# Macaron conv/attention layer step on one core: the first two weight tiles of the opening taken together, step by step

## The reference

```python
def rmsnorm(x, g):
    xf = x.astype(jnp.float32)
    y = xf * lax.rsqrt(jnp.mean(xf * xf, axis=-1, keepdims=True) + EPS)
    return (y * g.astype(jnp.float32)).astype(x.dtype)

def swiglu_ffn(x, norm_g, w_gu, w_down):
    h = rmsnorm(x, norm_g)
    g, u = jnp.split(h @ w_gu, 2, axis=-1)
    return (jax.nn.silu(g) * u) @ w_down

...
    x = x + 0.5 * swiglu_ffn(x, lw['norm_ffn1'], lw['ffn1_w_gu'], lw['ffn1_w_down'])
```

## Time and profile before

| | |
|---|---|
| median of 3 runs | 1531.73 us (1531.05 to 1533.61) |
| the profiled execution's own time | 1531.8 us |
| its span | 1530.0 us |
| PE busy | 1515.0 us, 99% of the span |
| DVE busy | 1031.8 us, 67% |
| ACT busy | 657.2 us, 43% |
| POOL busy | 663.8 us, 43% |
| mean granted PE clock | 0.997 |
| read from HBM | 118.31 MB |

### The profile page before, as it was taken

The page is one execution under the profiler, slowest core; times in us unless marked ns, Lnnn a source line. Parts: engine busy times, 40 slices in busy tenths (PEclk is TensorE's granted clock), DMA queues, the critical chain, the costliest instruction groups (busy, mean ns, idle before and its releaser), DMA issues.

```text
span 1530.0 us, 31753 instructions
## 1 busy us (share of the span) xinstructions
PE 1515.0 (99%) x11075; PEld 1465.3 (96%) x11075; DVE 1031.8 (67%) x1644; ACT 657.2 (43%) x1247; POOL 663.8 (43%) x679
## 2 busy tenths in 40 slices
PE   8999999999999999999999999999999999999999
PEld 8999999999999999588999999988999999999999
DVE  6998888422269975865877777864759988885000
ACT  6444345322221241364666666652434434445111
POOL 4165546445445644320233333223552654555432
PEclk9999999999999999999999999999999999999999
DMA  6233334232223341002322222312222333332322
GB/s 176 70 96 96 96 89 124 66 92 78 81 71 100 98 111 51 1 0 59 80 62 63 66 63 63 89 56 70 83 83 64 103 96 87 104 94 80 91 76 81
DMA packets 230911, 122.80 MB, mean 80 GB/s; under 512 B 28295, under 2 KB 227400, under 8 KB 230806
## 3 DMA queue, kind: packets, MB, share of 16 engines
q1 hardware_dynamic: 229950, 121.09, 28.2%
q10 hardware_dynamic: 864, 0.48, 0.1%
HBM read 118.31 MB, written 3.58 MB: 80 GB/s over the span
## 4 chain that ended last, share of the span: by engine, by line
PE 89%; DVE 5%; ACT 2%; issue 2%; POOL 1%; DMA 1%; SPq 0%; ACTq 0%; DVEq 0%; POOLq 0%
PE ps L498 39%; PE ps L1527 27%; PE ps L1907 10%; PE ps L1799 1%; PE ps L1670 1%; PE ps L1724 1%; PE ps L1699 1%; PE ps L1838 1%; PE ps L1817 1%; PE ps L1867 1%; PE ps L1818 1%; POOL w_lobuf L473 1%; PE ps L484 1%; PE ps L1714 1%; PE ps L1676 1%
## 5 line engine op out<-in xcount | busy, mean ns | idle before, releaser
L473 POOL TENSOR_TENSOR w_lobuf<-w_rawbuf,w_hibuf 128x256 fp32r<-128x256 f32 (+1 forms) x332 | 315.5, 981 | 360.3 <-ACT w_hibuf L466 360.2
L1527 PE MATMUL ps<-xs,w 128*128 128x288 f32 x3192 | 427.5, 296 | 1.9 <-DVE w L2033 1.9
L1527 PEld LDWEIGHTS ps<-xs,w 128*128 128x128 f32 x3192 | 426.8, 188 | 2.4 <-issue 2.4
L820 POOL TENSOR_TENSOR w<-w_raw,w 128x256 fp32r<-128x256 f32 x216 | 219.5, 1048 | 228.9 <-DVE w_raw L2021 149.8
L466 ACT ACTIVATE w_hibuf<-w_rawbuf 128x1024 fp32r<-128x1024 f32 (+1 forms) x89 | 104.4, 1173 | 345.9 <-PE ps L498 341.3
L2235 DVE SCALAR_TENSOR_TENSOR xT<-ps,xT 128x576 f32<-128x576 f32 x23 | 17.4, 757 | 202.4 <-PE ps L498 202.4
L498 PE MATMUL ps<-a_hi,w_lobuf 128*128 128x288 f32 x682 | 147.5, 298 | 0.0
L498 PE MATMUL ps<-a_hi,w_hibuf 128*128 128x288 f32 x682 | 147.1, 296 | 0.0
L498 PE MATMUL ps<-x_hi,w_hibuf 128*128 128x288 f32 x656 | 142.5, 299 | 4.3 <-POOL w_lobuf L473 2.5
L498 PE MATMUL ps<-a_lo,w_hibuf 128*128 128x288 f32 x682 | 145.4, 294 | 0.0
L498 PE MATMUL ps<-x_hi,w_lobuf 128*128 128x288 f32 x656 | 141.2, 297 | 0.0
(11 more groups left out here) (353 smaller groups left out, 2851.4 us busy)
## 6 DMA issues: line engine op xcount, KB each, us to landing
w_raw<-in_ffn_w_gu SPq DMA_DIRECT2D x76, 256.0 KB, 2.9
up_rows<-in_ffn_w_gu SPq DMA_DIRECT2D x72, 256.0 KB, 3.2
c_nat<-in_cache_ckv SPq DMA_DIRECT2D x128, 128.0 KB, 2.0
w_rawbuf<-in_w_in SPq DMA_DIRECT2D x58, 256.0 KB, 3.2
w_rawbuf<-in_ffn_w_down SPq DMA_DIRECT2D x32, 384.0 KB, 4.1
w_rawbuf<-in_ffn_w_down SPq DMA_DIRECT2D x32, 320.0 KB, 3.4
w_rawbuf<-in_ffn_w_gu SPq DMA_DIRECT2D x24, 256.0 KB, 3.4
w_rawbuf<-in_w_out SPq DMA_DIRECT2D x16, 256.0 KB, 3.1
```

What stands on the lines that cost most here:

```text
L473: ins = pool.tensor_tensor(w_lobuf[:, r, part], w_rawbuf[:, r, part], w_hibuf[:, r % HIS, part].bitcast(F32), ALU.subtract)
L820: ins = pool.tensor_tensor(w7[b][:, slot, 1, part], w7_raw[b][:, slot, 1, part], w7[b][:, slot, 0, part].bitcast(F32), ALU.subtract)
L1527: mm = pe.matmul(ps[:, seven_bank(f, slot), 0:HALF], m, xs[:, slot, n, k, :], start=k == 0 and j == 0, stop=k == KH - 1 and j == 2)
```

## The change

The first two weight tiles are loaded by halves (512 columns of `w_rawbuf`, the token tiles 0 to 3 of each): both first halves behind token tile 0, then token tiles 1 to 3. SP then waits until ACT has split both first halves (`x_root` at 2) before it issues the second halves, the token tiles 4 to 7 and all that follows. ACT splits by halves, after token tile 0 and after token tile 3. POOL makes the low parts of the first halves, two pieces for each tile in turn; DVE makes those of the second halves, 512 columns each, between its token tiles 3 and 4. PE takes, for each token tile, the six matmuls of the first weight tile and then the six of the second. The third tile's high part gets a place of its own (`third_hi`, at S1, free at that time); ACT makes it between the second and the third square, without the wait for `w_used`, and POOL and PE read it there. The numbers of `x_root` move up by four.

```diff
--- before.py
+++ after.py
@@ -253,6 +253,7 @@
         m_hi = place("m_hi", [P, KD, T], F32R, S1)
         m_lo = place("m_lo", [P, KD, T], F32R, S1 + XB)
         first_sq = place("first_sq", [P, 6, T], F32, A_AT)
+        third_hi = place("third_hi", [P, KD * P], F32R, S1)
         x_ss = place("x_ss", [P, NX], F32, A_AT + 24 * T)
         x_diag = place("x_diag", [P, NX, X_ROWS], F32, ta_at)
         early_rows = place("early_rows", [P, 2, KH * P], F32, S1 + 2 * XB)
@@ -485,13 +486,13 @@
                                    start=False, stop=i == len(kts) - 1 and j == 2)
             return mm
 
-        def product(pe, r, s, kts, hi, lo, width=P, w0=0, first=True, last=True, wait_k=None):
+        def product(pe, r, s, kts, hi, lo, width=P, w0=0, first=True, last=True, wait_k=None, w_hi=None):
 
             for i, k in enumerate(kts):
                 if wait_k:
                     wait_k(k)
                 off = (w0 + i) * width
-                wh = w_hibuf[:, r % HIS, off:off + width]
+                wh = (w_hibuf[:, r % HIS] if w_hi is None else w_hi)[:, off:off + width]
                 wl = w_lobuf[:, r, off:off + width]
                 for j, (a, b) in enumerate(((wh, hi), (wh, lo), (wl, hi))):
                     for h in range(2):
@@ -631,11 +632,23 @@
                 a, b = X_PARTS[i]
                 sp.dma_start(xT[:, a:b, :], xv[:, a:b, :]).then_inc(x_in[i], 16)
 
+            def load_half(n, col, h):
+
+                k = slice(h * KD // 2, (h + 1) * KD // 2)
+                dst = w_rawbuf[:, n, 0:KD * P].rearrange("p (k c) -> p k c", c=P)
+                sp.dma_start(dst[:, k, :], wv[:, k, col:col + P]).then_inc(w_in_sem[n], 16)
+
             load_tokens(0)
-            load_chunk(sp, 0, 0, wv, 0, KD, 0, P, wait=False)
-            for i in range(1, len(X_PARTS)):
-                load_tokens(i)
-            for n, col in ((1, DFF), (2, P), (3, P + DFF)):
+            load_half(0, 0, 0)
+            load_half(1, DFF, 0)
+            load_tokens(1)
+            load_tokens(2)
+            sp.wait_ge(x_root, 2)
+            load_half(0, 0, 1)
+            load_half(1, DFF, 1)
+            load_tokens(3)
+            load_tokens(4)
+            for n, col in ((2, P), (3, P + DFF)):
                 load_chunk(sp, n, n, wv, 0, KD, col, P, wait=False)
 
             def load_seven(f, wv, u, b):
@@ -803,14 +816,18 @@
                 for g in range(4):
                     split_lo(pool, n + g, (n0 + g) % RAWS, size)
 
-            for n in range(2):
-                pool.wait_ge(w_hi_done, n + 1)
-                for c in range(4):
-                    part = slice(c * KD * P // 4, (c + 1) * KD * P // 4)
+            for c in range(2):
+                for n in range(2):
+                    pool.wait_ge(x_root, n + 1)
+                    part = slice(c * 2 * P, (c + 1) * 2 * P)
                     pool.tensor_tensor(w_lobuf[:, n, part], w_rawbuf[:, n, part], w_hibuf[:, n, part].bitcast(F32), ALU.subtract)\
                         .then_inc(w_piece, 1)
-                pool.wait_ge(w_piece, 4 * n + 4)
-                pool.sem_inc(w_lo_done, 1)
+            pool.wait_ge(w_hi_done, 3)
+            for c in range(4):
+                part = slice(c * 2 * P, (c + 1) * 2 * P)
+                ins = pool.tensor_tensor(w_lobuf[:, 2, part], w_rawbuf[:, 2, part], third_hi[:, part].bitcast(F32), ALU.subtract)
+            ins.then_inc(w_lo_done, 3)
+
             def weights_lo(f, u, b):
 
                 for slot in G_LOW:
@@ -835,7 +852,7 @@
                     weights_lo(f, (i, 1), 1)
                     weights_lo(f, (i, 2), 0)
 
-            plain_lo(0, n_ffn1_up, 2)
+            plain_lo(0, n_ffn1_up, 3)
             sevens_lo(0)
             with pool.Fori(0, KD // 2) as i:
                 lo4(i * 4 + n_ffn1_down, n_ffn1_down, DK * P)
@@ -1066,15 +1083,24 @@
             act.wait_ge(ones_done, 1)
             act.activation(rstd[:, 0:P], ones[:, :], ACT.Sqrt)
             act.wait_ge(rows_in, 2 * 16)
+            def first_half(n, h):
+
+                part = slice(h * KD * P // 2, (h + 1) * KD * P // 2)
+                act.wait_ge(w_in_sem[n], 16 * h + 16)
+                act.activation(w_hibuf[:, n, part], w_rawbuf[:, n, part], ACT.Copy).then_inc(x_root, 1)
+
             for t in range(KD):
                 act.wait_ge(x_in[x_part(t)], 16)
                 act.activation(x2_hi[:, t, :], xT[:, t, :], ACT.Copy, scale=cols[:, G_FFN1 + t:G_FFN1 + t + 1]).then_inc(xh_done, 1)
-                if t == 0:
-                    split_hi(act, 0, 0, KD * P, free=False)
-            split_hi(act, 1, 1, KD * P, free=False)
+                if t in (0, 3):
+                    for n in range(2):
+                        first_half(n, t // 3)
+            act.sem_inc(w_hi_done, 2)
             for t in range(KD):
+                if t == 2:
+                    act.wait_ge(w_in_sem[2], arrived(2, 2))
+                    act.activation(third_hi[:, :], w_rawbuf[:, 2, 0:KD * P], ACT.Copy).then_inc(w_hi_done, 1)
                 if t == 6:
-                    split_hi(act, 2, 2, KD * P)
                     act.wait_ge(acc_done, 1)
                 act.activation(first_sq[:, t if t < 6 else t - 4, :], xT[:, t, :], ACT.Square).then_inc(sq_done, 1)
 
@@ -1109,7 +1135,7 @@
                         weight_hi(f, 0, 0, slot)
                     act.wait_ge(var_done, 2)
                     act.activation(x_ss[0:X_ROWS, :], x_ss[0:X_ROWS, :], ACT.Sqrt).then_inc(x_root, 1)
-                    act.wait_ge(x_root, 1)
+                    act.wait_ge(x_root, 5)
                     for g in range(NX):
                         act.activation(x_diag[0:X_ROWS, g, :], ident[0:X_ROWS, 0:X_ROWS], ACT.Copy, scale=x_ss[0:X_ROWS, g:g + 1])\
                             .then_inc(x_root, 1)
@@ -1439,19 +1465,16 @@
 
             pe.wait_ge(ones_done, 1)
             keep_busy(WARM, ps[:, 1, HALF:HALF + P])
-            def first_chunk(n, k):
-
-                pe.wait_ge(xl_done, k + 1)
-                pe.wait_ge(w_piece, 4 * n + k // 2 + 1)
-                mm = product(pe, n, n, range(k, k + 1), x2_hi, x2_lo, w0=k, first=k == 0, last=k == KD - 1)
-                if k == KD - 1:
-                    mm.then_inc(w_used, 1)
-
             def first_pair():
 
-                for n in range(2):
-                    for k in range(KD):
-                        first_chunk(n, k)
+                for k in range(KD):
+                    pe.wait_ge(xl_done, k + 1)
+                    for n in range(2):
+                        if k % 2 == 0 and k < KD // 2:
+                            pe.wait_ge(w_piece, k + n + 1)
+                        mm = product(pe, n, n, range(k, k + 1), x2_hi, x2_lo, w0=k, first=k == 0, last=k == KD - 1)
+                        if k == KD - 1:
+                            mm.then_inc(w_used, 1)
 
             def chunk(n, r, q, s, kts, hi, lo, width=P, first=True, last=True, wait_k=None, after_x=None):
 
@@ -1482,7 +1505,7 @@
 
                 third = T // 3 // X_ROWS
                 for g in range(NX):
-                    pe.wait_ge(x_root, g + 2)
+                    pe.wait_ge(x_root, g + 6)
                     mm = pe.matmul(stat0[:, g // third, g % third * X_ROWS:(g % third + 1) * X_ROWS], ones[0:X_ROWS, :], x_diag[0:X_ROWS, g, :],
                                    start=True, stop=True)
                 mm.then_inc(x_spread, 1)
@@ -1553,11 +1576,11 @@
                 else:
                     first_pair()
                     pe.wait_ge(w_lo_done, 3)
-                    product(pe, 2, (q_up + 2) % 4, range(0, 2), x2_hi, x2_lo, last=False)
+                    product(pe, 2, (q_up + 2) % 4, range(0, 2), x2_hi, x2_lo, last=False, w_hi=third_hi)
                     first_sums()
-                    product(pe, 2, (q_up + 2) % 4, range(2, 6), x2_hi, x2_lo, w0=2, first=False, last=False)
+                    product(pe, 2, (q_up + 2) % 4, range(2, 6), x2_hi, x2_lo, w0=2, first=False, last=False, w_hi=third_hi)
                     first_spread()
-                    product(pe, 2, (q_up + 2) % 4, range(6, KD), x2_hi, x2_lo, w0=6, first=False).then_inc(w_used, 1)
+                    product(pe, 2, (q_up + 2) % 4, range(6, KD), x2_hi, x2_lo, w0=6, first=False, w_hi=third_hi).then_inc(w_used, 1)
                     chunk(3, 3, q_up + 3, (q_up + 3) % 4, range(KD), x2_hi, x2_lo)
                 for n in (4, 5):
                     pe.wait_ge(plain_lo_done, 2 * f + n - 3)
@@ -2043,6 +2066,11 @@
                 dve.wait_ge(xh_done, t + 1)
                 dve.scalar_tensor_tensor(x2_lo[:, t, :], xT[:, t, :], cols[:, G_FFN1 + t:G_FFN1 + t + 1], x2_hi[:, t, :].bitcast(F32),
                                          op0=ALU.mult, op1=ALU.subtract).then_inc(xl_done, 1)
+                if t == 3:
+                    rest = slice(KD * P // 2, KD * P)
+                    for n in range(2):
+                        dve.wait_ge(x_root, n + 3)
```

(1 more changed line is left out.)

## The result

The changed kernel takes **1534.91 us** in the median of 22 runs (1532.08 to 1536.01); the kernel before took 1531.87 in 22 runs of the same session (1528.35 to 1534.88). The ratio is 1.0019, 95% interval 1.0013 to 1.0024: some 3 us slower, outside the range of 1529.2 to 1533.3. The interval is 1.7 us wide, so this many runs tell apart less than the 3.1 us that the prediction reckoned with. The profiled execution took 1533.31 us, one of the quickest of the 22; why it flatters the change is told at the end.

The account below looks back on a forecast made before the run. PE is busy 99% of the span, but DVE's x_ss sets the end: a removed wait gives 1.6 us, later adds take 2.1, fewer contending pieces give 0.8, so 0.3 us earlier, 1531.5 against 1531.8; range 1529.2 to 1533.3.

Parts of the forecast that it names:

- Part 2: Loads on SP: released at 6.9 us, first half lands at 10.0, last tokens at 14.0 instead of 11.5.
- my upper bound of 15.4: Latest landing of the last tokens, if the first half takes the loaded queue's 4.5 us.
- Rival 2: Slow refill of the load queue: last tokens at 15.4, x_ss at 30.2, time 1532.9 us; chance 0.2.
- Part 1: Joint first pair on PE: ends at 21.0 instead of 22.6, 1.6 us less; DVE's two subtractions hidden.
- Part 3: Squares on ACT, adds on DVE: first square at 15.4, first add at 18.8 against 16.73, 2.1 us later.
- Part 4: DVE's eight operations before x_ss: 10.0 us, six POOL pieces costing 0.38 each; DVE reaches x_ss at 28.8.
- rival 3: POOL's pieces block DVE outright, each costing 0.72 us: 1.7 us lost, time 1533.5 us; chance 0.05.
- Part 5: Third weight tile: POOL's low part ends by 23.4, not 24.65; PE's sums free x_ss by 27.8, no longer last.
- The frame: Opening up to PE's resumption at 69.46: the kernel's end moves by as much as x_ss moves on DVE.

Follow-up runs that it names:

- e1: The change without SP's wait, the second halves counted on semaphores of their own: median 1530.89 us, ratio to before 0.9996.
- e9: The change with SP's wait kept, but token tiles 4 to 7 issued ahead of it, only second weight halves and later weight tiles behind: 1529.73 us, 0.9981.
- e11: The change without SP's wait, token tiles 4 to 7 loaded ahead of the second weight halves, run a second time: 1529.88 us, 0.9986.
- e10: Repeat of e2, the kernel before with the added SP wait alone: 1532.98 us, ratio 1.0007.
- e2: The kernel before with one SP wait added ahead of token tiles 4 and 5, until ACT has split the first weight tile: 1533.36 us, 1.0012.
- e7: e1 with PE's joint order undone, first weight tile over all eight token tiles, then the second: 1531.38 us, 0.9989.

## Why the prediction was wrong, step by step

**The step that failed is Part 2, "the two token parts at 12.45 and 14.0 (1.55 each ...)".** Its first half is right: release 6.83 (6.9 forecast), the first weight half 3.1 us after its issue, as the earlier trace rows had it, the second at 11.1 (10.9). Issues of the change at 6.83 and 7.79 (KB, us to landing):

```profile
w_rawbuf<-in_ffn_w_gu SPq DMA_DIRECT2D x1, 256.0 KB, 3.1
...
xT<-in_x_t SPq DMA_DIRECT2D x1, 576.0 KB, 7.0
```

I then let the tokens flow behind the halves at the rate of a full queue. The second dip is what I left out: 14.8 and 16.4 instead of 12.45 and 14.0, 2.4 us, and above even my upper bound of 15.4, which priced a slow first load and full speed behind it. Rival 2 named the mechanism (tokens late behind SP's wait, all else sliding), with a price that was 1.0 us short on the landing (15.4) and 2.0 on the time (1532.9); I gave it 0.2 because "an idle queue answered in 3.1 us", a row about a load with only one other, of 256 KB, behind it. The 2.0 us of fixed cost that the Trainium skill gives (DMA: Bandwidth & Descriptors, "Anatomy of one DMA"; on GpSimd's path) fits the first dip: estimated 2.9 us for the first half, measured 3.1. It says nothing of the second, and by it the forecast would have been no better.

The other steps, with the tokens at 16.42 put in:
- *Part 1*: the first pair ended at 23.2, late with its tokens. In e1, where they land at 13.3, it ended at 21.1 (forecast 21.0), and PE's cover held: in the change the two DVE subtractions took 1.46 us inside a wait for tokens.
- *Part 3*: the first square 1.38 us after landing (1.45 forecast), the first add 3.37 behind it (3.40): 21.17 is 18.8 plus the 2.4 us.
- *Part 4*: from the first add to `x_ss` 10.5 us, 10.0 forecast (and 10.0 in e1). Seven pieces met DVE instead of six: three of the third tile, as forecast, but all four of the fourth. The excess is 2.8 us, 0.40 for each (0.38 assumed). So a piece does not cost DVE its whole 0.72 us, as rival 3 had it. But this does not speak against a lock, as the prediction took it to. In the rows after the change DVE's sums and POOL's pieces keep one beat: a sum starts every 1.14 us (27.10, 28.25, 29.39), and four pieces take 4.62. One after the other, a sum and a piece take 1.32 alone: 0.60 from one sum to the next (e9, below) and 0.72. So for most of their length they take turns. The Trainium skill (SBUF — State Buffer, "Who interferes with whom") has the shared pair as an exclusive lock held for the whole instruction. The trace nearly agrees with that rule (1.14 of 1.32 us). The sums in e9, where no POOL piece ran beside them up to 25.0 us:

```profile
23.79 0.68 DVE L2040 TENSOR_TENSOR w_raw<-early_rows 128x512 f32<-128x512 f32 x1
24.39 0.68 DVE L2042 TENSOR_TENSOR w_raw<-w_raw,early_rows 128x512 f32<-128x512 f32 x1
25.00 0.68 DVE L2044 TENSOR_TENSOR w_raw<-w_raw 128x512 f32<-128x512 f32 x1
```

- *Part 5*: the sums left DVE free (28.0 to 29.5, `x_ss` at 31.7): right, and here DVE was that late.
- *The frame*, "the end moves by as much as `x_ss` moves", held within 0.4 us: `x_ss` +2.6, PE's resumption +3.0, the medians +3.0. Against the forecast (`x_ss` 28.8, so PE's resumption at 69.2) 2.4 us come from the landing, 0.5 from Part 4 and 0.4 from DVE's stop behind `x_ss`, 3.3 together. Over the table the median less PE's resumption is 1462.0 to 1462.4 us in ten of the fourteen rows; outside are e9 (1461.7), e11 (1461.3), e10 (1461.1) and e2 (1464.0), where the one profiled execution need not be like the median run.

Told as two terms: from the last landing to `x_ss` the change needs 15.3 us instead of 17.6, a gain of 2.3 (forecast 2.8: 28.8 less 14.0); the landing itself is 4.9 later (forecast 2.5). e9 keeps the first and drops most of the second. Which of the change's parts brings the gain (POOL's pieces given to DVE, the third tile's own place) was not taken apart further; PE's order does not (14.7 us from landing to `x_ss` with it, e1, and 14.8 without, e7).

## What to carry to other kernels

Cost a wait in a load queue by what the queue still holds when the wait ends, and not by the wait's length: here token loads issued 4 us before the queue came to them ran at full rate, those issued 2 us before did not. Put the loads that the critical chain needs ahead of such a wait, and the others behind it. A row of how fast an idle queue answers prices the first load behind a gap (3.1 us, forecast and measured), and not the loads behind that one.

## What the runs showed that was not expected

- **A second dip.** A drained queue did not only start late; 1 us after it had filled again, the transfers fell to a fifth of their rate for the packets of loads issued about 2 us before (67 GB/s at the lowest, against 289 to 437 from 9.7 us on with the wait ended at 4.0). All 16 DMA engines had to finish, and the last one was 1.8 us behind the median one at the last landing (0.5 in e1 and in the kernel before). What delays these packets the runs do not show.
- **The end of a profile can mislead by 1.7 us and more.** PE is busy for 19.7 to 20.0 of the 20 us from 700 to 720, as in the 10 us before (9.7 to 10.0), yet is granted the lower level, 1.2 GHz, for a part of it that differs from execution to execution. That stretch in the kernel before, the change and e1:

```profile
700.00:720.00 20.00, 20.00 (x146) 19.48 (x144) 10.79 (x19) 8.15 (x14) 1.80 (x1) 0.83 0.19 49
```

```profile
700.00:720.00 20.00, 19.66 (x157) 18.98 (x157) 10.45 (x21) 9.70 (x19) 1.80 (x1) 0.91 0.25 67
```

```profile
700.00:720.00 20.00, 20.00 (x132) 19.48 (x131) 10.06 (x18) 7.65 (x14) 1.80 (x1) 0.74 0.19 49
```

A mean of 0.83 over 20 us is 6.8 us at the half level ((1 − 0.83) × 20 / 0.5), 0.91 is 3.6 us, 0.74 is 10.4. At that level PE begins fewer matmuls (146, 157 and 132 in the three stretches, in step with the clock), so half of that time, 3.4, 1.8 and 5.2 us, is an estimate of the loss. The profiled times less PE's resumption differ by about so much: 1462.3, 1460.8 and 1463.8 us. Thus the change's profiled execution is only 1.5 us above that of before, while its opening, and the medians, are 3.0 apart; and e1's is above before's, while its median is below. For a change in the opening, the opening's own readings were the better measure.
